# Other order of the first weight copies, of the sample's queries and of the turned queries and keys, and ten unused products, in a one-core hybrid encoder step

## The reference

```python
h = rmsnorm(x, norm_g)
proj = einsum('btd,de->bte', h, w_in)          # rq rk rv rg | aq ak av ag | iq ik iw
ro = retention(rope(rq), rope(rk), rv, state)  # 4 heads of 128, chunks of 64 frames
ro = rmsnorm(ro, ret_gn_g) * silu(rg)
index = sum_h relu(iq_h . ik) * iw_h           # 8 heads of 64; masked by chunk
sel = top_k(index, 256)                        # keys per query
ao = softmax(aq . ak[sel] / 8) @ av[sel]       # 8 heads of 64, 2 key/value heads
ao = ao * silu(ag)
y = rmsnorm(x + concat(ro, ao) @ w_out, final_g)
```

## Time and profile before

| what | before |
|---|---|
| median of 3 runs | 833.62 us (830.43 to 833.85) |
| the profiled execution: its own time | 833.51 us |
| its span in the trace | 832.0 us |
| mean granted clock of TensorE | 0.976 |
| TensorE busy, matmuls | 768.7 us, 92% |
| TensorE busy, weight loads | 645.9 us, 78% |
| VectorE busy | 484.2 us, 58% |
| ScalarE busy | 336.8 us, 40% |
| GpSimd busy | 167.2 us, 20% |
| DMA, mean | 96 GB/s |

### The profile page before, as it was taken

One profiled execution on the slowest core, in us unless ns is written; L12 is line 12 of the kernel. 1 busy time (PEld: TensorE's weight loads), 2 busy tenths in 40 slices (PEclk: granted clock), 3 DMA queues, 4 the chain that ended last, 5 costly groups with the idle time before them and its releaser, 6 DMA issues.

```text
span 832.0 us, 12279 instructions
## 1 busy us (share of the span) xinstructions
PE 768.7 (92%) x4157; PEld 645.9 (78%) x4157; DVE 484.2 (58%) x1188; ACT 336.8 (40%) x759; POOL 167.2 (20%) x361
## 2 busy tenths in 40 slices
PE   6799989899989899988899999999999999999993
PEld 5688868787878878867788787888788788888882
DVE  6543687979787897879747332333475523332244
ACT  5655565757566575657462111111245200101110
POOL 1332314131302113020203122222231111100111
PEclk9998999999989999989999999999999999999997
DMA  9620030303012011021446212121476632333331
GB/s 274 230 84 23 26 114 18 114 10 105 19 51 102 9 58 36 27 77 51 141 125 179 71 69 69 69 69 69 157 229 191 190 87 96 106 101 126 126 102 38
DMA packets 36863, 79.80 MB, mean 96 GB/s; under 512 B 13712, under 2 KB 14880, under 8 KB 35536
## 3 DMA queue, kind: packets, MB, share of 16 engines
q1 hardware_dynamic: 29968, 59.81, 22.7%
q0 software_dynamic: 6416, 19.31, 7.4%
q10 hardware_dynamic: 432, 0.09, 0.1%
HBM read 58.67 MB, written 20.53 MB: 95 GB/s over the span
## 4 chain that ended last, share of the span: by engine, by line
PE 57%; DVE 18%; ACT 8%; issue 7%; DMA 7%; POOL 2%; SPq 0%; DVEq 0%; ACTq 0%; POOLq 0%
PE bank L904 39%; DVE probs L1771 3%; PE bank L1077 3%; PE bank L923 3%; DVE work L1622 2%; PE bank L1066 2%; DVE w_lo L1516 2%; DMA xT<-turned_x 2%; PE bank L936 2%; DMA early<-in_w_in 2%; DMA stage<-in_w_out 2%; DVE idx L1603 1%; ACT w_hi L1216 1%; PE bank L1004 1%; ACT pT L1325 1%
## 5 line engine op out<-in xcount | busy, mean ns | idle before, releaser
L904 PE MATMUL bank<-w_hi,xT 128*128 128x512 f32 (+1 forms) x1040 | 335.6, 392 | 7.5 <-DVE xT L1549 3.6
L904 PEld LDWEIGHTS bank<-w_hi,xT 128*128 128x128 f32 x1040 | 194.4, 190 | 50.4 <-DMA xT<-turned_x 4.8
L904 PE MATMUL bank<-w_lo,xT 128*128 128x512 f32 (+1 forms) x520 | 200.2, 385 | 0.0
L904 PEld LDWEIGHTS bank<-w_lo,xT 128*128 128x128 f32 x520 | 98.9, 190 | 17.3
L1077 PE MATMUL bank<-v_sb,pT 128*128 128x64 f32 x648 | 90.4, 277 | 6.5 <-ACT pT L1325 6.4
L1077 PEld LDWEIGHTS bank<-v_sb,pT 128*128 128x128 f32 x648 | 84.6, 198 | 11.3 <-ACT pT L1325 10.6
L904 PE MATMUL bank<-w_hi,mT 128*128 128x512 f32 x256 | 82.8, 397 | 1.3 <-DVE w_lo L1516 1.3
L1325 ACT COPY pT<-bank 128x384 f32<-128x384 f32 (+3 forms) x108 | 50.7, 476 | 75.5 <-PE bank L1066 74.1
L1066 PE MATMUL bank<-ident,probs 128*128 128x128 f32 x324 | 55.8, 285 | 18.8 <-ACT probs L1314 18.3
L1314 ACT ACTIVATE probs<-probs,low 128x128 f32<-128x128 f32 (+8 forms) x68 | 54.5, 802 | 27.9 <-DVE low L1771 27.9
L1066 PEld LDWEIGHTS bank<-ident,probs 128*128 128x128 f32 x324 | 38.9, 149 | 29.2 <-ACT probs L1314 26.9
(11 more groups left out here) (225 smaller groups left out, 1223.2 us busy)
## 6 DMA issues: line engine op xcount, KB each, us to landing
xT<-turned_x SPq DMA_DIRECT2D x34, 512.0 KB, 4.1
stage<-in_w_in SPq DMA_DIRECT2D x40, 256.0 KB, 2.9
turned_x<-xT SPq DMA_DIRECT2D x9, 1024.0 KB, 5.2
xin<-in_x_prompt SPq DMA_DIRECT2D x16, 256.0 KB, 3.8
y_row<-in_x_prompt SPq DMA_DIRECT2D x16, 256.0 KB, 5.1
stage<-in_w_out SPq DMA_DIRECT2D x16, 256.0 KB, 3.1
out<-y_row POOLq DMA_DIRECT2D x16, 256.0 KB, 2.4
early<-in_w_in SPq DMA_DIRECT2D x3, 1024.0 KB, 7.9
```

The lines of the kernel that those rows point to most:

```text
L904: mm = pe.matmul(out, (lo if which == 2 else hi)[:, k, :], (w_lo if which == 1 else w_hi)[slot][:, k, 0:width], start=(i == 0), stop=(i == ...
```

## The change

Four edits.

1. SP issues the two `aq` copies ahead of the load of tile 1's frames.
2. `keep_busy` takes a count and a weight. Before the first `turn` of tile 0 two products of `w_hi` of `iq` are made, and before that of tile 7 eight of `w_hi` of `rq` (as many blocks as `rq` has; they wait until VectorE has split the last of them). They go into the bank that the `turn` overwrites, and nobody reads them.
3. The copy of the sample's `aq` product goes from the head of tile 7's list into `index(8)`, ahead of the copies of the folded index. The second exponential of tile 7 no longer stands ahead of the loop over the heads; the loop puts it behind the first head's two `turn` steps. POOL turns (rotates) the sample's `aq_row` ahead of the guess of the threshold, as for all other tiles.
4. `between_heads(t)` puts the step `turn` behind head 4 where the tile has two groups (tiles 4 to 6, since tile 7 has no t+2), else behind head 5 as before; and `copy_order` holds ScalarE's copies for two further `turn` steps everywhere, where it was three with two groups.

```diff
-BETWEEN_HEADS = {1: "kv", 5: "turn"}
+def between_heads(t):
+    return {1: "kv", 4 if len(groups_of(t)) > 1 else 5: "turn"}
...
         order += [("exp", 1, 0), ("between", "iq", t + 2)]
-        exps = 2
-    elif t + 1 == SAMPLE:
-        order += [("exp", 1, 0), ("between", "aq", SAMPLE)]
         exps = 2
...
-            held.append([step, 3 if step[1] == "turn" and len(groups_of(t)) > 1 else 2])
+            held.append([step, 2])
...
+FIRST_TURN = {0: (2, "iq"), NT - 1: (8, "rq")}
...
             load_early("kv")
+            load_early("aq")
             load_x(1)
-            load_early("aq")
...
-            def keep_busy(key):
+            def keep_busy(key, n=WARM, w="iq"):
                 wait_free(pe, key)
-                for k in range(WARM):
-                    pe.matmul(of(key)[:], w_hi[SLOT["iq"]][:, k, 0:P], w_hi[SLOT["iq"]][:, k, 0:BW], start=True, stop=True)
+                if w == "rq":
+                    pe.wait_ge(w_split, split_no[w, KD - 1])
+                for k in range(n):
+                    pe.matmul(of(key)[:], w_hi[SLOT[w]][:, k, 0:P], w_hi[SLOT[w]][:, k, 0:BW], start=True, stop=True)
...
                     elif kind == "turn":
+                        if (h, n) == (0, 0) and t in FIRST_TURN:
+                            keep_busy(key, *FIRST_TURN[t])
                         pe.wait_ge(exped, AH * t + h + 1)
...
                     if t == SAMPLE:
+                        between("aq", SAMPLE)
...
-                if t != SAMPLE:
-                    rotate_aq(t)
+                rotate_aq(t)
                 if searched(t):
                     guess_threshold(t, no)
...
-                if t == SAMPLE:
-                    rotate_aq(t)
```

More of the change, by code:

```diff
@@ L140, in attention_order @@
             order += scores(h + held)
-        if t + 2 < TILES and h in BETWEEN_HEADS:
-            if BETWEEN_HEADS[h] == "kv":
+        if t + 2 < TILES and h in between_heads(t):
+            if between_heads(t)[h] == "kv":
                 order.append(("exp", exps, 0))
                 exps += 1
-            order.append(("between", BETWEEN_HEADS[h], t + 2))
+            order.append(("between", between_heads(t)[h], t + 2))
         elif t + 2 >= TILES:
```

## The result

The changed kernel takes 837.42 us (median of 11 runs, 836.23 to 839.44) against 833.62. The ratio of their executions is 1.0054, 95% interval 1.0044 to 1.0064: 4.5 us slower, where 2 us faster was predicted; the time lies outside the range. The profiled execution took 837.96 us (span 836.4), 4.45 more than that of before.

What follows compares the result with a forecast made beforehand. TensorE was taken as the bound (57% of the chain), with VectorE the bound in tile 7. Terms -1.6 + 0.5 + 0 - 1.25 + 0.4 = -1.95 against 833.51 gave 831.6 us, range 828.3 to 835.2.

Steps and rivals of the forecast that it cites:

- Turn one head sooner: Tiles 4 to 6: head 6's exponential delayed, wait at tile's end gone; +0.1 per tile, +0.4 us in all.
- rival 1: Tiles 0 and 7: the extra products hold TensorE's clock up, winning 2.2 us more, time 829.4 us; chance 0.2.
- First copies: Start: aq issued ahead of x(1) lands near 20.4, work behind it moves forward; -1.6 us.
- Two products: Tile 0: two unused products before the first transposition, with no wait to hide them, cost +0.5 us.
- Tile 7: Eight products fit in TensorE's wait, 0; ScalarE's new order removes VectorE's wait for head 2's scores, -1.25 us.
- Rival 2: Start or tile 7: one of the two wins (1.6 or 1.25 us) is missing, 833.0 us; chance 0.2.
- Rival 3: Tiles 4 to 6: ScalarE's copies before head 6's exponential cost in full, 4.9 us, time 836.1; chance 0.13.

Runs made afterwards that it cites:

- run 3: Changed kernel plus five unused TensorE products ahead of head 6's first transposition in tiles 4 and 5; 831.88 us, ratio 0.9996.
- run 1: Changed kernel with the turn step and ScalarE's copy order of tiles 4 to 6 put back as before; 830.45 us, ratio 0.9984.
- run 5: Kernel before with only the two aq copies moved ahead of tile 1's frames; 831.06 us, ratio 0.9973.
- run 6: Changed kernel with the old turn place and copy order in tiles 4 to 6 and without the ten unused products; 830.81 us, ratio 0.9972.
- run 8: Changed kernel with the old turn place and copy order, plus five unused products ahead of heads 3 and 4 of tile 7; ratio 0.9972.
- run 2: Kernel before with only the earlier turn step and its copy order in tiles 4 to 6; 838.07 us, ratio 1.0069.
- run 11: Kernel before, ScalarE repeating one head 5 copy eight times more in tile 4, six in tile 5, delaying head 6's exponential; 842.84 us, ratio 1.0119.
- run 9: Kernel before, ScalarE repeating one head 5 copy five times more in tile 4, four in tile 5, delaying head 6's exponential; 836.1 us, ratio 1.0035.
- run 10: As run 9, plus five unused TensorE products ahead of head 6's first transposition in tiles 4 and 5; ratio 1.0024.
- run 4: Changed kernel with ScalarE's copies of turned queries and keys in tiles 4 to 6 held for three turns, not two; 842.71 us, ratio 1.0127.
- run 12: As run 11, plus five unused TensorE products ahead of head 6's first transposition in tiles 4 and 5; 839.02 us, ratio 1.0063.

## Why the prediction was wrong

**The step that failed** is the sum of "Turn one head sooner": "Per tile +1.1 - 1.0 = 0.1", +0.4 in all. Its walk was right. The transposition of head 6 came 1.2 us later in tile 5, measured against what stands ahead of it (from 285.85 to 286.32, while the transposition before it went from 282.38 to 281.68), as the 1.0 to 1.2 said; the wait at the tile's end went. With the clock kept up (run 3) tiles 4 to 6 cost 155.51 against 155.0 without the edit (mean of runs 1, 5, 6 and 8): +0.5, where +0.4 was predicted; those four have a clock of 0.97 to 1.00 in tiles 4 and 5, so this compares nearly like with like. What was left out is what 1.45 and 1.77 us of idling do to TensorE: two stretches of 10.2 us at 1.2 GHz. So the edit cost 161.35 - 155.0 = 6.3 us by the rows of run 2, in place of 0.4. Part of this the kernel before had paid already, in slow stretches of its own, so that the whole change lost 4.4 there.

The prediction did name the mechanism, in rival 1, for the edit that fills a wait, and gave it only the sign of a win. It read the new waits of tiles 4 and 5 as delays that are given back, though the earlier trace rows showed the clock at half in tiles 0 and 7, where TensorE had waited. Not every wait of the kernel before has such a stretch behind it: the clock is 1.00 from 287.4 to 297.6, which holds the wait of 1.03 in the earlier trace rows. The Trainium skill, page "TensorE: Matmul & The Clock Gate", section "HAM oscillation — how this bites in real kernels", has a case of this kind: a matmul loop that waits for its copies between bursts begins each burst on the half clock, with longer waits than those of TensorE that are named here. Runs 2, 3 and 11 agree with it, for shorter waits; run 9 and the wait of 2.73 us in run 6 do not. The prediction quoted it for the eight products only.

**First copies: right.** `aq` was predicted at 20.4 and came at 19.59. The first index scores started at 31.62 before and at 29.75 after; the kernel before had a slow stretch ahead of them, from about 24 to 26, so the 1.87 us are not the copies' alone. Then 1.5 us were given back in the stretch at half clock from 34.8, which lies in dense products. Run 5 gives -0.27% (-0.44 to -0.10), 2.3 us; the term was 1.6.

**Two products: right.** They take from 62.72 to 63.18, 0.46 us; +0.5 was predicted. They bought nothing: slow stretches near 71 came with them (runs 1 and 3) and without (run 5), and stayed away with them (the change) and without (run 2).

**Tile 7: right in its rows.** -1.25 predicted; 51.42 against 52.60 is -1.18, and the eight products cost 0. The time of the whole kernel does not show the win (runs 5 and 6). In the change itself tile 7 took 52.88, with a slow stretch from 386 in which TensorE is busy all of the time.

**Rivals.** Rival 1's fall of the clock was the cause, with the other sign. Rival 2 is half true in the change's own execution, where the win of tile 7 is missing. Rival 3 had the place and nearly the size (836.1), for another reason: ScalarE's copies did not cost their 4.9 us, the clock did.

## What to carry to other kernels

A step moved ahead of another engine's critical instruction must be priced twice: by the delay, and by the wait that it opens on TensorE, since behind that wait the next dense work may run at half clock. Where a wait can't be removed, matmuls that nobody reads, in a bank that is overwritten anyway, can be worth far more than they cost: ten of them won back 5.6 us of three tiles in run 3. In tile 7, in tile 0, and in run 10, where the clock had not fallen without them, they won nothing. And slow stretches are to be weighed by their place: the change has as much time at half clock as the kernel before had in its profiled execution, and is 4.45 us slower.

## What was not expected of the hardware

The clock's fall does not follow from the length of one wait: behind 1.06 and 1.40 us (run 9) and 2.73 (run 6) it stayed at 1.00; behind 1.04 (the end of tile 4 in run 8), 1.45 and 1.77 (the change), 1.38 (tile 6 of run 4, with 1.58 soon after) and 2.28 and 2.43 (run 11) it fell. Tile 7 of the change has two waits of 1.54 us: behind the first, at 379.79, the clock stayed at 1.00, behind the second, at 385.09, it fell. Run 3 shortens the waits and adds work to TensorE at once, so it can't tell which of the two holds the clock. Which of the slow stretches near 35, 71 and 108 us appear differs between executions of kernels that are alike there: the kernel before and runs 9 to 12 are alike up to the end of tile 3, and reach it between 189.61 and 191.96 us. What decides between the cases is left open.
